# One wait for free slots per four picks in an expert gather, a down ring of eight slots, and four kept queries

## What is computed

```python
q = (xt @ w_q).reshape(T, PEER_HEADS, 2, PEER_QDIM // 2)
s1 = jnp.einsum('thd,hnd->thn', q[:, :, 0], sub_keys[0]).astype(jnp.float32)
s2 = jnp.einsum('thd,hnd->thn', q[:, :, 1], sub_keys[1]).astype(jnp.float32)
# top 16 of each, top 16 of their 256 sums: `expert`, and `gate` = softmax of the 16
def per_block(args):
    x_blk, e_blk, g_blk = args
    u = w_down[e_blk]
    a = jnp.einsum('td,ted->te', x_blk, u).astype(jnp.float32)
    hg = (jax.nn.gelu(a, approximate=False) * g_blk).astype(w_up.dtype)
    return jnp.einsum('te,ted->td', hg, w_up[e_blk]).astype(x_blk.dtype)
```

## Time and profile before

| what | value |
|---|---|
| median of three runs | 3121.55 us |
| the profiled execution, its own time | 3136.85 us |
| its span | 3135.1 us |
| PE busy | 2725.9 us (87%) |
| DVE busy | 2011.3 us (64%) |
| ACT busy | 1305.2 us (42%) |
| POOL busy | 1073.1 us (34%) |
| granted clock of TensorE, mean | 0.933 |

### The profile page before, as it was taken

The page is one execution under the profiler, slowest core; times in us unless marked ns, Lnnn a source line. Parts: engine busy times, 40 slices in busy tenths (PEclk is TensorE's granted clock), DMA queues, the critical chain, the costliest instruction groups (busy, mean ns, idle before and its releaser), DMA issues.

```text
span 3135.1 us, 44731 instructions
## 1 busy us (share of the span) xinstructions
PE 2725.9 (87%) x14826; PEld 2204.2 (70%) x14826; DVE 2011.3 (64%) x3647; ACT 1305.2 (42%) x2197; POOL 1073.1 (34%) x1355
## 2 busy tenths in 40 slices
PE   8998799899899978999997699998965787777776
PEld 8986699799789866999996578887753333333222
DVE  6665467576566655577779955555857666666654
ACT  4446444444444454544447645544542222212111
POOL 4422344144144200000005500000006777777774
PEclk9999899999999988999998899998987888999888
DMA  9973399699589742555551055555428999999996
GB/s 343 372 255 123 108 361 366 206 340 376 187 313 377 241 160 77 173 183 184 181 181 54 0 178 192 193 193 180 167 80 335 371 356 383 363 373 355 372 363 259
DMA packets 217334, 773.94 MB, mean 247 GB/s; under 512 B 29600, under 2 KB 29600, under 8 KB 216336
## 3 DMA queue, kind: packets, MB, share of 16 engines
q0 software_dynamic: 118192, 411.91, 35.1%
q1 hardware_dynamic: 99040, 360.75, 33.6%
HBM read 704.39 MB, written 68.16 MB: 246 GB/s over the span
## 4 chain that ended last, share of the span: by engine, by line
PE 52%; POOL 11%; DVE 6%; issue 6%; DMA 4%; ACT 2%; DVEq 0%; ACTq 0%; POOLq 0%; SPq 0%
PE ps L1508 15%; PE ps L1509 14%; PE ps L1510 14%; POOL arena L398 6%; PE ps L1876 6%; POOL arena L394 5%; DMA arena<-down_rows,arena 3%; DVE first_hot L1451 1%; PE ps L1656 1%; PE ps L1554 1%; DVE arena L1382 1%; DVE second_hot L1454 1%; DVE arena L1463 1%; DVE w_lo L903 0%; ACT arena L537 0%
## 5 line engine op out<-in xcount | busy, mean ns | idle before, releaser
L903 DVE TENSOR_TENSOR w_lo<-raw,w_hi 128x1024 fp32r<-128x1024 f32 x681 | 831.6, 1224 | 644.0 <-ACT w_hi L502 639.0
L502 ACT ACTIVATE w_hi<-raw 128x1024 fp32r<-128x1024 f32 x681 | 719.1, 1056 | 650.0 <-PE ps L1510 430.0
L1508 PE MATMUL ps<-act_hi,w_hi 128*128 128x256 f32 x2728 | 780.6, 286 | 40.3 <-DVE w_lo L903 21.1
L1509 PE MATMUL ps<-act_lo,w_hi 128*128 128x256 f32 x2728 | 774.4, 284 | 0.0
L1510 PE MATMUL ps<-act_hi,w_lo 128*128 128x256 f32 x2728 | 774.3, 284 | 0.0
L1876 PE MATMUL ps<-arena 128*128 128x512 f32 x1024 | 522.1, 669 | 177.3 <-ACT arena L655 177.3
L1508 PEld LDWEIGHTS ps<-act_hi,w_hi 128*128 128x128 f32 x2728 | 525.8, 193 | 49.5 <-issue 28.6
L1876 PEld LDWEIGHTS ps<-arena 128*128 128x128 f32 x1024 | 214.7, 215 | 473.7 <-issue 257.6
L1509 PEld LDWEIGHTS ps<-act_lo,w_hi 128*128 128x128 f32 x2728 | 526.1, 193 | 5.6 <-issue 2.4
L1510 PEld LDWEIGHTS ps<-act_hi,w_lo 128*128 128x128 f32 x2728 | 525.8, 193 | 0.0
L1382 DVE SCALAR_TENSOR_TENSOR arena<-arena 128x1024 f32<-128x1024 f32 x256 | 313.9, 1227 | 258.2 <-DMA arena<-down_rows,arena 257.2
(11 more groups left out here) (243 smaller groups left out, 3033.6 us busy)
## 6 DMA issues: line engine op xcount, KB each, us to landing
raw<-in_stream SPq DMA_DIRECT2D x684, 512.0 KB, 3.4
arena<-in_stream POOLq DMA_DIRECT2D x128, 512.0 KB, 8.7
down_rows<-arena POOLq DMA_DIRECT2D x512, 128.0 KB, 5.8
pad<-in_ln POOLq DMA_DIRECT2D x4, 1024.0 KB, 6.4
arena<-down_rows,arena POOLq DMA_INDIRECT x256, 6.2
arena<-in_stream,arena POOLq DMA_INDIRECT x256, 6.3
arena<-in_subkeys POOLq DMA_DIRECT2D x2, 1024.0 KB, 5.9
x<-in_x SPq DMA_DIRECT2D x1, 1024.0 KB, 5.1
```

The source lines that it names most:

```text
L502: act.activation(w_hi[:, u % SPLIT, :], raw[:, u % RAW, :], ACT.Copy).then_inc(hi_done, 1)
L903: dve.tensor_tensor(w_lo[:, u % RAW, :], raw[:, u % RAW, :], w_hi[:, u % SPLIT, :].bitcast(F32), ALU.subtract).then_inc(lo_done, 1)
L1508: pe.matmul(dst, lhs[0], rhs[0], start=first, stop=False, **kw)
L1509: pe.matmul(dst, lhs[0], rhs[1], start=False, stop=False, **kw)
```

## The change

POOL no longer waits before each pick but before each fourth one (`p % ISSUE == 0`), for both rings at once and ahead of the down gather: for the dots of all but the last four picks issued, and for the matmuls of all but the last eight. Then it issues four picks, eight gathers, with no wait. The down ring grows from 6 to 8 slots; the up ring keeps 12. Of the 16 queries four are kept in a ring, and the areas of the arena move to make room for the two new slots.

```diff
-DOWN_RING, UP_RING, DIAG_RING = 6, 12, 8
-E_INDEX, E_DIAG, E_DOWN, E_UP, E_XP = 6144, 6400, 7424, 13568, 25856
+ISSUE, Q_KEPT = 4, 4
+DOWN_RING, UP_RING, DIAG_RING = 2 * ISSUE, 3 * ISSUE, 8
+E_QUERY, E_INDEX, E_DIAG, E_DOWN, E_UP, E_XP = 3072, 6144, 6400, 7424, 15616, 1024
@@
-                        if p >= DOWN_RING:
-                            pool.wait_ge(dot_done, p - DOWN_RING + 1)
+                        if p % ISSUE == 0 and p >= DOWN_RING:
+                            pool.wait_ge(dot_done, p - DOWN_RING + ISSUE)
+                        if p % ISSUE == 0 and p >= UP_RING:
+                            pool.wait_ge(up_used, p - UP_RING + ISSUE)
                         pool.indirect_dma_start(down_in[:, p % DOWN_RING, :], None, down_rows[:, :],
                                                 at).then_inc(down_row[p % DOWN_RING], 16)
-                        if p >= UP_RING:
-                            pool.wait_ge(up_used, p - UP_RING + 1)
                         pool.indirect_dma_start(up_in[:, p % UP_RING, :], None, stream_rows, at,
                                                 element_offset=UP_1 * P * UNIT).then_inc(up_row[p % UP_RING], 16)
@@
-                    act.activation(area(E_Q + T * u, T), ps[:, 4 + u % 2, 0:T],
+                    act.activation(area(E_QUERY + T * (u % Q_KEPT), T), ps[:, 4 + u % 2, 0:T],
                                    ACT.Copy).then_inc(query_kept, 1)
@@
-                    queries, keys = blk(E_Q, 16), blk(E_SK, 16, NK)
+                    queries, keys = blk(E_QUERY, Q_KEPT), blk(E_SK, 16, NK)
@@
-                                                queries[:, 2 * h + f, P * b:P * b + P], keys[:, 2 * h + f, :],
+                                                queries[:, (2 * h + f) % Q_KEPT, P * b:P * b + P], keys[:, 2 * h + f, :],
```

## The result

The changed kernel takes 3251.07 us (median of four runs, 3249.08 to 3255.87), the kernel before 3119.81 us beside it: a ratio of 1.0425, 95% interval 1.0394 to 1.0455, 131 us slower. The forecast was 3198 us with a range up to 3235 us. Its direction and its mechanism hold; its size falls short by 53 us. The profiled execution has a span of 3249.9 us against 3135.1 us.

What follows compares the result with a forecast made beforehand. POOL's own gather issuing was taken to set the last stage, 11.51 us a batch. A 25.5 us round for two batches adds 1.24 us to each of 61, 76 us: median 3121.55 to 3198 us, range 3142 to 3235 us.

Steps and rivals of the forecast that it cites:

- Waits taken away, ring of eight, four queries: Gather stage: fewer met waits, a down ring of eight and four kept queries each bring 0 us.
- The loop of two batches: New up wait on POOL ties batch m to batch m - 2; half a round per batch, 76 us lost over 61 batches.
- The size of the round: Gather stage: one round for two batches takes 25.5 us, 12.75 us a batch against POOL's own 11.51 us.
- six steps of issue: POOL, from batch start to issue of its fourth down gather: 8.65 us, kept as before.
- landing: Fourth down gather's arrival after issue: 6.08 us, kept as before.
- to the first matmul, with exponential: Weights, diagonal matrices and first matmul 0.58 us, plus 0.3 us a round for the exponential once per item.
- sixteen matmuls: PE, a group's matmuls: 8.58 us, nearly all groups at the lower clock rather than 7.13 us.
- last matmul to gather: POOL's start after the releasing matmul: no term in the round, so 0 us.
- the slower loop rules: Rival: even batches' loop, round about 26.4 us, holds the odd ones too; +103 us, 3225 us; chance 0.15.
- Hidden pauses: Rival: transfers set the gather stage, queued gathers cover POOL's 1.3 us pauses; no change, 3122 us; chance 0.06.
- Warm matmuls: Rival: PE's gaps stay under 3 us, rounds of 24.0 us; +31 us, 3153 us; chance 0.13.
- Shorter rounds: Rival: emptied DMA queue lands the fourth down gather sooner, round 21.5 us; 46 us gained, 3075 us; chance 0.06.

Runs made afterwards that it cites:

- up_per_pick: Changed kernel with only the up-ring wait put back to each pick, behind the down gather; 3125.94 us, ratio 0.9997 to the kernel before.
- down_first: Changed kernel with the batched up wait behind the first down gather of the batch instead of ahead of it; 3196.06 us.
- fewer_products: Changed kernel leaving out half the up rows' product for two of four picks, 12 matmuls a group instead of 16, timing only; 3200.45 us.
- no_lag: Changed kernel with each group's weighing, diagonals and matmuls right after its own last dot; 3141.89 us, ratio 0.9965 to the kernel before.
- issue_2: Changed kernel with one wait per two picks, rings still 8 and 12; 3167.28 us, ratio 1.0057 to the kernel before.
- one_wait: Changed kernel without the wait on the dots where there is an up wait; 3243.22 us, ratio 1.0379 to the kernel before.
- after_again: Changed kernel, unedited, run again on another chip; 3246.5 us, ratio 1.0285 to the kernel before (3157.18 us there).
- up_ring_16: Changed kernel with 16 up slots, down ring of 6 with per-pick waits; 3106.21 us, ratio 0.9933; on another chip 3153.05 us, ratio 1.0013.

## Why the prediction was right and wrong

**Waits taken away, ring of eight, four queries: nothing.** Right: `up_per_pick` is 0.9997 of the kernel before.

**The loop of two batches.** Right in its path. The place, the lines it would show in and the half-round for each batch were as written. The pattern was not: instead of 1 to 2 us at nearly every batch and 70 to 100 us in total, POOL mostly waits 3 to 7.5 us at every second one, 144.5 us in total. `down_first`, `fewer_products`, `no_lag` and `issue_2` each change one piece of it, and the time followed: within 2 us of the expected time for the first, 4 us short of the expected gain for the second, inside the expected ratio for the other two.

**The size of the round: this step failed.** Means over the 31 odd and 30 even batches from the fourth on, worked out from the trace's rows, against the sum:

| term, us | sum | even | odd |
|---|---|---|---|
| six steps of issue | 8.65 | 8.23 | 8.49 |
| landing | 6.08 | 6.32 | 6.37 |
| dot | 1.33 | 1.39 | 1.34 |
| to the first matmul, with exponential | 0.88 | 0.78 | 0.77 |
| sixteen matmuls | 8.58 | 9.22 | 7.90 |
| last matmul to gather | 0 | 1.00 | 2.05 |
| round | 25.5 | 26.9 | 26.9 |

The miss of 1.4 us a round is 0.7 us a batch, 44 us over 61 batches; the sum's 76 us and these 44 make 120 us, and the stage grew by 118.9 us. It has three parts.

First, the restart. The sum let POOL start at the end of the last matmul, and put this term at 0 without a reason. It starts 0.76 us later when it is late, 0.27 us with one wait instead of two (`one_wait`). That was a cost of the added wait which the trace before showed in part: its own late gathers stood 0.27 us behind their matmuls. (The even column has 1.00 because four of its 30 batches are not late.)

Second, the matmuls. The sum took 8.6 us from groups behind gaps of 4 to 6 us. The late loop makes its own gaps, mostly of 6 us and more, and its groups take 9.2 us in the mean, up to 10.2. The rule of the Trainium skill that the forecast weighed ("TensorE: Matmul & The Clock Gate", section "HAM oscillation — how this bites in real kernels"), that waits between bursts of matmuls put each burst back to half rate, agrees with the groups behind these gaps: its price was put too low. The groups of the other loop take 7.9 us, so that the mean of both, some 8.5 us, is near what the sum had. These two terms are partly balanced by the issue, which takes 0.4 us less than in the sum.

Third, the tie. The sum took one round for all batches. The odd loop needs only 8.49 + 6.37 + 1.34 + 0.77 + 7.90 + 0.76 = 25.6 us, but its batches come on POOL's queue behind the eight gathers of the late one. (From batch 53 on the two change places; the means mix both stretches.) It is held to 26.9 us: the rival "the slower loop rules", which had 0.15. That it was put below the mean was the wrong choice. Its own price, 103 us, was near the 119 us of the stage.

**The forecast time.** 3198 us fell short of 3251 by 53 us. The 44 us above are most of it. The other 9 come from carrying the sum over from one execution to the median: the profiled execution before was 15 us above its median, and the forecast took this off, but that of the changed kernel is only 0.7 us above. Against this, the parts outside the stage are 4 us shorter in the changed kernel's trace. Measured against the kernel before of another chip the loss is 89 us (`after_again`), because that kernel is slower there by 37 us and this one isn't. The loss is thus not one number. The changed kernel stays at 3246 to 3251 us on its two chips, with stages of 854.1 and 854.5 us and none of the long stands, while the time of the kernel before moves with the chip. That it stays because waits between engines set its pace was expected before the run and fits, but the reason is not shown.

**The rivals.** *Hidden pauses* fell: the rate went from 369 to 318 GB/s with the pauses, and what the Trainium skill ("DMA: Bandwidth & Descriptors", section "Where 436 GB/s comes from") gives as the bound of one core, about 358 GB/s, is not one here, with 412 GB/s over 4 us in the stand shown above. *Warm matmuls* fell: groups of 7.1 us are 26 of 64. *Shorter rounds* fell: the fourth down gather of a batch lands after 6.2 us in the median after pauses as well; the first one comes down most, to 4.3 us, and it isn't the one that the round runs over.

## What to carry to other kernels

A wait for a whole batch on a ring asks, at its first pick, for what the last pick would have needed: subtract the batch from the ring and see whether the consumer's lag still fits in what is left. Here 12 slots less 4 were two batches, and the consumer was two batches and some 2.5 us behind (mean over the trace of the kernel before). Write the loop out, with the restart of the waiting engine as a term; where two loops share an engine, price the slower one, not the mean. If the lag can be shortened (`no_lag`, a few lines), this pays on either kernel. And measure two kernels side by side on one chip: here the chip alone moved a kernel by up to 1.5%.

## What was not expected of the hardware

- A gather behind two waits, the second of them late, starts 0.76 us after the release; behind one wait 0.27 us (21 of 22 late batches in `one_wait`).
- A gather's descriptors take up to 1.05 us longer if it starts during a dot of two SBUF tensors, and hardly at all (945 to 968 ns each) if one is in PSUM. But faster issuing brought no time: POOL stood some 4 us at a time, and the transfers dropped to 202 GB/s.
- After a pause the transfers come back slowly. In the round shown they had run out (2 GB/s from 2947 to 2949 us) and then moved 255 GB/s over 4 us though POOL issued one gather in 1.245 us, against 409 to 413 GB/s in undisturbed stretches.
- The same gather-bound kernel took 3120 to 3157 us on different chips. In the two traces of `up_ring_16` the difference of 34 us lies wholly in the gather stage: 27 us of pauses, most with every slot free, and 7 us of longer issuing. What makes POOL stand there is open.
